# A hybrid decoder trunk on one core: meta queries left out, LayerNorm steps moved between engines, sample attention in float32r

## The reference, cut to what matters

```python
hp = concatenate([meta, x_prompt])         # 16 meta rows + 1024 prompt rows
hs = x_sample                              # 8 sequences x 8 new rows
# layer 0: pooling mixer, LN, SwiGLU, LN    layer 1: MLA, LN, SwiGLU, LN
def latent_attention(q_lat, q_pe, rows, q_pos, k_pos):
    c_kv, k_pe = rows[:, :256], rows[:, 256:]
    s = (q_lat @ c_kv.T + q_pe @ k_pe.T) * SCALE   # masked by position
    p = softmax(s)
    return p @ c_kv
# prompt: 1040 keys, 8 heads;  sample: 1024 cached rows (8 pages of 128) + 8 new ones per sequence
def mla_out(o_lat, w_uv, w_o): return (o_lat @ w_uv).reshape(n, t, 1024) @ w_o
def swiglu(h, w_gate, w_up, w_down): return (silu(h @ w_gate) * (h @ w_up)) @ w_down   # 1024 -> 2816 -> 1024
hp = LN(ALPHA * hp + mix); hp = LN(ALPHA * hp + swiglu(hp))      # the same for hs
return hp[:, 16:], hs, new states and latent cache rows
```

## Time and profile before

| what | us |
|---|---|
| median of the runs | 2528.48 |
| lowest run | 2527.64 |
| the profiled execution | 2538.14 |
| its span, first to last instruction | 2536.2 |
| TensorE busy | 2444.3 |
| VectorE busy | 1094.5 |
| GpSimd busy | 675.6 |
| ScalarE busy | 546.2 |

### The profile page before, as it was taken

The page is one execution under the profiler, slowest core; times in us unless marked ns, Lnnn a source line. Parts: engine busy times, 40 slices in busy tenths (PEclk is TensorE's granted clock), DMA queues, the critical chain, the costliest instruction groups (busy, mean ns, idle before and its releaser), DMA issues.

```text
span 2536.2 us, 36520 instructions
## 1 busy us (share of the span) xinstructions
PE 2444.3 (96%) x13475; PEld 2143.2 (85%) x13475; DVE 1094.5 (43%) x2030; ACT 546.2 (22%) x988; POOL 675.6 (27%) x448
## 2 busy tenths in 40 slices
PE   8999999999999979899999999989999999999996
PEld 8899999999999958587888884459999999999995
DVE  4443344334434562444555464423434433443446
ACT  3411111111111253232232223523111111111112
POOL 3532222322222330111112100333222322323225
PEclk9999999999999989999999999979999999999998
DMA  5111110111111010100000004511111011101111
GB/s 193 51 39 48 50 50 25 50 50 44 30 50 50 25 45 16 35 18 18 18 17 18 9 9 122 170 34 37 39 50 50 25 50 50 50 25 50 50 33 71
DMA packets 132430, 117.88 MB, mean 46 GB/s; under 512 B 8880, under 2 KB 119432, under 8 KB 132336
## 3 DMA queue, kind: packets, MB, share of 16 engines
q1 hardware_dynamic: 132352, 116.83, 14.8%
HBM read 110.94 MB, written 6.42 MB: 46 GB/s over the span
## 4 chain that ended last, share of the span: by engine, by line
PE 89%; DVE 4%; ACT 2%; issue 1%; ACTq 0%; DVEq 0%; POOL 0%
PE ps L682 23%; PE ps L683 23%; PE ps L684 22%; PE ps L1027 3%; PE ps L931 2%; PE ps L1014 1%; PE ps L1111 1%; PE ps L903 1%; PE ps L945 1%; PE ps L1086 1%; PE ps L936 1%; PE ps L977 1%; PE ps L1070 1%; DVE BNS L1484 1%; PE ps L980 1%
## 5 line engine op out<-in xcount | busy, mean ns | idle before, releaser
L682 PE MATMUL ps<-XH,WGH 128*128 128x368 f32 x2112 | 697.8, 330 | 4.0 <-DVE XL L1514 2.4
L683 PE MATMUL ps<-XL,WGH 128*128 128x368 f32 x2112 | 698.2, 331 | 0.0
L684 PE MATMUL ps<-XH,WGL 128*128 128x368 f32 x2112 | 695.8, 329 | 0.0
L1596 DVE TENSOR_TENSOR XR<-XR,ps 128x512 f32<-128x512 f32 x756 | 510.8, 686 | 8.3 <-PE ps L684 4.5
L1579 DVE TENSOR_TENSOR HF<-SG,ps 128x368 f32<-128x368 f32 x132 | 71.0, 538 | 917.7 <-PE ps L684 906.1
L682 PEld LDWEIGHTS ps<-XH,WGH 128*128 128x128 f32 x2112 | 397.2, 188 | 8.1 <-DVE XL L1514 2.8
L683 PEld LDWEIGHTS ps<-XL,WGH 128*128 128x128 f32 x2112 | 396.7, 188 | 1.9
L684 PEld LDWEIGHTS ps<-XH,WGL 128*128 128x128 f32 x2112 | 396.9, 188 | 0.0
L684 PE MATMUL ps<-WDH,HL 128*128 128x512 f32 (+1 forms) x792 | 313.5, 396 | 0.0
L682 PE MATMUL ps<-WDH,HH 128*128 128x512 f32 (+1 forms) x792 | 310.7, 392 | 2.0 <-DVE XR L1596 2.0
L683 PE MATMUL ps<-WDL,HH 128*128 128x512 f32 (+1 forms) x792 | 312.0, 394 | 0.0
(11 more groups left out here) (216 smaller groups left out, 2965.3 us busy)
## 6 DMA issues: line engine op xcount, KB each, us to landing
RAWG<-ffn_w_gate SPq DMA_DIRECT2D x44, 512.0 KB, 5.9
RAWG<-ffn_w_up SPq DMA_DIRECT2D x44, 512.0 KB, 6.9
RAWD<-ffn_w_down SPq DMA_DIRECT2D x44, 512.0 KB, 3.4
CR<-cache_mla_l SPq DMA_DIRECT2D x64, 160.0 KB, 2.6
XR<-x_prompt SPq DMA_DIRECT2D x8, 512.0 KB, 12.3
WOR<-mla_w_o SPq DMA_DIRECT2D x8, 512.0 KB, 3.2
WOA<-mla_w_o SPq DMA_DIRECT2D x1, 4096.0 KB, 17.2
o_y_prompt<-XR SPq DMA_DIRECT2D x8, 512.0 KB, 2.6
```

Source lines behind the costliest of these rows:

```text
L682: pe.matmul(out, w[0], x[0], start=start, stop=False)
L683: pe.matmul(out, w[0], x[1], start=False, stop=False)
L684: return pe.matmul(out, w[1], x[0], start=False, stop=stop)
L1596: dve.tensor_tensor(XR[0:r, t, ds], XR[0:r, t, ds], ps[0:r, 4 + 2 * w + half, :], ALU.add).then_inc(s_row[2 * l + 1], 1)
```

## The change

It does the following.

- **Meta queries.** The eight units of block 8 are gone; every head has eight units in one `ORDER`, with a new `NEXT_PLAN` and positions for GpSimd's work. The meta columns of `OT8` are zero.
- **Second FFN.** `turned`, `columns` and `third` put the sample rows at columns 1024 to 1087; the last third has 352 columns. The down products of tile 8 still have 80 rows.
- **LayerNorm.** After the first FFN GpSimd scales and shifts all nine tiles. Tile 8 of the LayerNorm behind the attention goes to VectorE. At the end VectorE takes tiles 6, 7, 8 whole, from the raw rows, in two fused operations a tile, behind its other work. The rows of tile 1 are normalized ahead of an FFN step that stood before them.
- **Sample attention.** Queries stand twice in 128 rows. Probabilities are split into a high part (ScalarE) and a low part (VectorE), side by side in 128 columns; the latents of the pages into a high copy `CH` (ScalarE) and a low part in place (GpSimd). The value product is 18 float32r matmuls of 256 columns; two matmuls with `IIF` (the identity twice) add the halves and transpose. The loop over steps is written out.
- **Order.** Pages of the first two sequences are loaded during attention. Page transposes of the first sequence stand between the first ten last output products, the other six stand in the sample tail. The first third of FFN unit 0 comes ahead of the sample output product. `w_o` is loaded head by head during the steps.

```diff
-LN_VECTOR = ((3, 6), (2, 5, 8), (), (2, 5, 8))
+LN_VECTOR = ((3, 6), (), (8,), (6, 7, 8))
 FIRST_TRANSPOSES = (({(1, 7): 6}, {(0, 5): 7, (1, 3): 8}, {}),
-                    ({(0, 1): 3, (0, 2): 4, (0, 5): 5, (1, 0): 6, (1, 3): 7}, {(0, 2): 8}, {}))
+                    ({(0, 6): 3}, {(1, 7): 8}, {}))
-        ORDER = ((7, 8, 6, 0, 5, 1, 4, 2, 3), (0, 7, 8, 6, 3, 5, 1, 4, 2))
+        ORDER = (7, 0, 6, 3, 5, 1, 4, 2)
...
+        FIRST_LAST, TAIL_SIDE = LAST_SIDE[:10], LAST_SIDE[10:]
+        def columns(l, t):
+            return slice(SEQ - META, SEQ + NS) if l == 1 and t == NT - 1 else cols(t)
+        def third(l, j):
+            return slice(j * TW, min(j * TW + TW, TOK - l * META))
+        def turned(k, t):
+            if k == 2 and t == NT - 1:
+                return slice(META, TAIL), slice(SEQ, SEQ + NS)
+            return slice(0, rows(t)), cols(t)
...
 # SP
+            load_pages(0, slot(0))
+            sp.wait_ge(h_s, NQ * (H - 1))
+            load_pages(1, slot(1))
+            sp.wait_ge(h_pv, NU)
+            load_pages(2, slot(2))
...
 # TensorE, sample_outputs
-                for k in range(NPAGE):
-                    pe.matmul(ps[0:NS, 6, 0:KVL], PST[:, k, :], CR[:, b, k, 0:KVL], start=(k == 0), stop=False)
+                for k in range(NPAGE + 1):
+                    if k in (0, NPAGE // 2, NPAGE):
+                        pe.wait_ge(c_nl, 3 * s + 2 * k // NPAGE + 1)
+                    high = CH[:, s % 2, k, :] if k < NPAGE else NRH[:, s % 2, :]
+                    low = CRL[b][:, k, 0:KVL] if k < NPAGE else NRL[:, b, :]
+                    pe.matmul(ps[:, 6, 0:KVL], PST[:, k, :], high, start=(k == 0), stop=False)
+                    ins = pe.matmul(ps[:, 6, 0:KVL], PST[:, k, :], low, start=False, stop=(k == NPAGE))
...
 # TensorE, second FFN
                 for j in range(3):
                     pe.wait_ge(s_xl, 2 * NT * l + 3 * j + 3)
                     gate_up_unit(l, 0, True, j, FIRST_TRANSPOSES[l][j])
+                    if l == 1 and j == 0:
+                        sample_product()
...
+            def sample_product():
+                pe.wait_ge(c_ov, 1)
+                pe.wait_ge(c_wo, 16 * H)
+                for half in (0, 1):
+                    ... # 16 passes each, as before, into banks 1 and 3
+                    if half == 0:
+                        ln_transposes(2, 4)
+                        ln_transposes(2, 5)
+                ins.then_inc(c_wm, 1)
+                ln_transposes(2, 6)
+                ln_transposes(2, 7)
+                pe.wait_ge(s_row[2], 1)
...
+            for s, between, behind in ((NSEQ - 2, TAIL_SIDE[0:2], TAIL_SIDE[2:3]),
+                                       (NSEQ - 1, TAIL_SIDE[3:5], TAIL_SIDE[5:6])):
                 probability_transposes(s)
+                for f in between:
+                    side(f)
+                sample_outputs(s, slot(s))
+                for f in behind:
+                    side(f)
                 sample_out_transposes(s)
...
 # ScalarE, sample_step
+                latents_high(s, 0, slot(s))
+                sample_probabilities(s, slot(s))
                 evacuate_pages(act, copy, s + 1, 4).then_inc(c_xa, 1)
+                if s > 0:
+                    sample_rows(s - 1, slot(s - 1))
+                latents_high(s, 1, slot(s))
+                if s in (0, 3):
+                    norm_rows([0] if s == 0 else [1, 2, 3])
...
 # VectorE
+            def ln_whole(k, t):
+                dve.scalar_tensor_tensor(XR[0:r, t, :], XR[0:r, t, :], MV[0:r, t, 0:1], GB[0:r, 0, :], ALU.subtract,
+                                         ALU.mult).then_inc(s_lv, 1)
+                ...
+                dve.scalar_tensor_tensor(XR[0:r, t, :], XR[0:r, t, :], RS[0:r, t:t + 1], GB[0:r, 1, :], ALU.mult,
+                                         ALU.add).then_inc(s_lv, 1)
+                if k == 3 and t == NT:
+                    for u in ln_vector(k):
+                        ln_whole(k, u)
...
+            ln_low(2, 3)
+            hidden_unit(1, 0, True, 0)
+            ln_low(2, 4)
+            ln_low(2, 5)
             dve.wait_ge(c_wm, 1)
+            ... # add the sample product to tile 8, its statistics
+            ln_low(2, 6)
+            ln_low(2, 7)
+            ln_scales(2, NT - 1, TAIL, NT - 1)
+            ln_gain(2, NT - 1)
+            ln_low(2, NT - 1)
 # GpSimd
+            for s in range(NSEQ):
+                latents_low(s, slot(s))
+                if s == NSEQ - 1:
+                    gate_up_low(1, 0, 0)
+                    gate_up_low(1, 0, 1)
+                ln_pool(2, POOL_TILES[s])
```

More of the change, by code:

```diff
@@ L212, in slot @@
         def slot(s):
-            return (s + 1) % 3
+            return s % 3
         def bank2(b, r, n=1024):
@@ L763, in gate_up_unit @@
                 pe.wait_ge(f_hf[l], 3 * n + j + 1)
-                cs = slice(j * TW, (j + 1) * TW)
+                cs = third(l, j)
+                n_cols = cs.stop - cs.start
                 for m, done in ((0, f_gmm[l]), (1, f_umm[l])):
@@ L1455, in _ @@
                 sample_queries(s, slot(s))
-            sample_step(0, 0)
-            with act.Fori(0, 2) as j:
-                for k in (1, 2, 3):
-                    sample_step(j, k)
+            for s in range(NSEQ - 1):
+                sample_step(s)
             for s in (NSEQ - 2, NSEQ - 1):
@@ L1599, in swiglu @@
             def swiglu(l):
-                hidden(l, 0, True)
+                for j in range(l, 3):
+                    hidden_unit(l, 0, True, j)
                 dve.wait_ge(s_xr, NT * (2 * l + 1))
@@ L1788, in sample_step @@
-                if not first:
+                if s < 5:
+                    ln_statistics(2, s, P, s)
+                if s > 0:
                     sample_columns(s - 1)
-                if k % 3 == 0:
-                    for n in (range(1) if first else range(1, 4)):
-                        ln_scales(2, s - k + n, P, slot(n))
-            dve.wait_ge(h_fd, len(SIDE_DVE))
-            for k in (1, 3, 5):
-                evacuate_pages(dve, copy, 0, k).then_inc(c_xd, 1)
-            sample_step(0, 0)
@@ L1821, in _ @@
-            for t in range(3, NT):
-                ln_low(2, t)
+                if s in (0, 3):
+                    for t in ([0] if s == 0 else (1, 2, 3)):
+                        ln_scales(2, t, P, t)
+            dve.wait_ge(c_kn, 1)
+            dve.tensor_tensor(IIF[:], IDF[:, 0:NS], IDF[:, NS:2 * NS], ALU.add).then_inc(c_ii, 1)
+            for n, f in enumerate(FIRST_LAST):
+                side_dve(f)
+                if n in PAGE_AFTER and PAGE_AFTER.index(n) % 2 == 1:
+                    evacuate_pages(dve, copy, 0, PAGE_AFTER.index(n)).then_inc(c_xd, 1)
@@ new lines, in _ @@
+            for s in range(NSEQ - 1):
+                sample_step(s)
+            sample_maxima(NSEQ - 1, slot(NSEQ - 1))
+            probabilities_low(NSEQ - 2)
+            sample_sums(NSEQ - 1, slot(NSEQ - 1))
+            for f in TAIL_SIDE[0:3]:
+                side_dve(f)
+            sample_columns(NSEQ - 2)
+            probabilities_low(NSEQ - 1)
+            for f in TAIL_SIDE[3:6]:
+                side_dve(f)
+            ln_statistics(2, 5, P, 5)
+            sample_columns(NSEQ - 1)
```

469 lines of the change are left out of this document (258 added, 211 removed).

## The result

The changed kernel takes 2489.81 us (median of 4 runs, 2489.32 to 2490.36), the kernel before 2529.18 beside it (four executions, one of them of 8561.45, the others 2527.64 to 2529.88). The ratio is put at 0.9826 with an interval of 0.9805 to 0.9847; the two medians alone give 0.9844, inside it. The kernel is faster, by a little less than 2%. Forecast were 2477.0, with a range of 2460 to 2495.

The account below looks back on a forecast made before the run. TensorE, busy 2444.3 of 2536.2 us, was taken as the bound. Seven terms summed to 51.5 us, giving 2486.6 for the profiled execution and 2477.0 for the median, with a range of 2460 to 2495.

Parts of the forecast that it names:

- case A: Whole kernel: the terms as summed give 2477 us, own range 2469 to 2486; chance 0.5.
- Rival C: After the first FFN: GpSimd becomes the bound, term 3 is -7 us, time 2490; chance 0.12.
- rival B: Tail: it keeps its gaps and low clock, term 6 is 0, time 2492; chance 0.2.
- term 2: Attention: eight of 72 units, the meta units, go; 7.4 us gained, bounds 3 and 9.
- term 5: Sample steps: cheaper float32r value products, a step from 15.40 to about 13.6 us; net 6.5 us gained.
- term 6: Tail, last sample scores to end of first gate/up block: 87.0 us becomes 72, 15 gained, bounds 0 and 20.
- Term 3: After the first FFN: GpSimd takes VectorE's scale and shift of three tiles; 6 us gained, bounds 0 and 11.
- Term 1: Second FFN: gate and up products lose 16 of 368 columns in the last third; 7.6 us gained.
- term 4: Start of the sample part: six page transposes move to the tail and gaps are filled; 5.5 us gained.
- term 7: End: VectorE sheds tiles 2 and 5, then runs six fused operations in 11.5 us; 3.5 us gained.
- Rival D: Sample steps: TensorE's clock falls to 1.2 GHz, steps double, +109 us, time 2601; chance 0.03.

Follow-up runs that it names:

- third tail run: Changed kernel with sequence 7's columns before tile 5's statistics, tile 0's transposes before the value-up product, half the sample output product before second-FFN unit 0: 2479.93 us.
- three tail runs: Changed kernel with VectorE's sequence 7 columns earlier, 2487.96 us; besides, tile 0's transposes earlier, 2485.03; besides, half the sample output product earlier, 2479.93.
- plan run: Changed kernel with the same side products of heads 1 to 6 spread otherwise over a head's eight units: 2475.83 us, ratio 0.9786.
- last version: Changed kernel with both the side products of heads 1 to 6 spread otherwise and the tail's new order in three places: 2465.68 us, ratio 0.9741.

## Why the prediction was right, and where it was not

The time lay in the range, 12.8 us above the forecast; it lay outside the 2469 to 2486 of case A, the sum, and by its number next to C's 2490 and B's 2492, of which C did not come and B came in part. That the kernel would stay within 2% of the one before had been given 0.47. Four of seven terms were near; of the three that missed, two nearly cancel (11.3 us too much in term 2, 8.2 too little in term 5), and that is luck.

**The base of the sum failed first.** The step "I make the sum against 2538.14 and take the same difference off the median" treats the 9.7 us as an offset that stays. They were low clock in the tail of that one execution, and term 6 counted them as gained: of the 12.8 us above the forecast they are 9.7. Against the execution for which it was made the sum, 2486.6, is 2.9 us off, and the tail gives 11.7; in an execution near the median it has 2.0 to give and not 15.

**Term 6, the tail (15, measured 2.0).** The work was priced well: 59.6 us forecast, 67.67 us busy in 75.1 with low clock, 61.2 without it (the third tail run). Besides the base, "I add 3 for low clock" is what failed: the stretch of 17.9 us was granted 0.52, which by these two busy times cost some 6.5 us; gaps were 7.4 us of the 9.4 forecast. Of rival B the low clock came and the gaps did not, and the three tail runs show what the clock hangs on in the changed kernel: with the waits filled by transposes and half a sample product, 9.9 us come back. The bound of 20 is a slip: 87.0 less 59.6 and half of 9.4 is 22.7. The gap feared ahead of the last third of unit 0 is 0.86 us.

**Term 2, the meta units (7.4, measured -3.9).** Work of 6.3 us did go. Outside even the lower bound of 3, "if half of that cover is missed", lies what happened: the prediction looked for exponentials that need cover, and the cover that was missing was for VectorE emptying two banks. The plan run shows it. The upper bound, that a new order of side products closes gaps, was the right idea: this order opened gaps, and that of the plan run closed them; with the work saved its attention is 10.7 us shorter than the kernel's before.

**Term 5, the sample steps (6.5, measured 14.7).** "A step goes from 15.40 to about 13.6" is where it was mis-sized: 12.64. The value products' saving was priced right (2.2 less 0.3 and 0.1, measured 1.55 for the pages alone). Missed was that one shape of operand throughout is cheaper: 0.58 a step is shown by the run with 64 columns; the other 0.6 lies by the timelines in the page transposes (0.59 to 0.35 for four, of which float32 brought back 0.09), and that was not run by itself. The "about 4.3 us" for which TensorE was to wait for ScalarE came to some 2 us more than before.

**Term 3 (6, measured 9.5).** Scale and shift alone are 5.8 at the latent product and 7.2 in the time. Most of the rest is the meeting of VectorE and GpSimd, which tile 1's new place, an unpriced move, avoids: against the execution of the kernel before in which VectorE started first (916.58) the shift is 6.5, near the forecast. Rival C, GpSimd as the bound, did not come: no wait for GpSimd's rows after the FFN. The rule against the move that the prediction weighed (the Trainium skill, page "GPSIMD Engine Reference", section "Engine selection") has the price right: 2.40 against 1.21 and 1.22 where VectorE is not held up (the run that gave scale and shift back), and 1.49 in the mean of the earlier trace rows. What decided was that GpSimd had the time and VectorE had not.

**Terms 1, 4 and 7** were 7.3 for 7.6 (21 of the 22 units lie in that stage), 6.0 for 5.5 and 3.6 for 3.5. Term 1 stands on the 7 ns in the timeline, term 4 on the stage alone; neither was run by itself. For term 7 the split was as forecast: two operations at the high price, four at the low. Its sum does not follow from its prices: two or three at 3.25 and the others at 1.49 are 12.5 to 14.2 us and not the 11.5 written. Measured are 11.7, because the low price turned out 1.27 to 1.34, so the hit is in part luck. Rival D did not come: 1.00 was granted in all steps, with waits of up to 1.0 us in them.

## What to carry to other kernels

Profile the kernel before twice: where two executions of one program differ, the stage that differs is not a stable term, and its low clock may not be there to gain. When short units of work are left out, look at what they stood between: two products into one bank need as much other work between them as the other engine takes to get to it and empty it. A wait that can't be shortened is worth filling with work that is due anyway, since what runs behind it may run at half the clock.

## What the runs showed of the hardware

- In the run with 64 columns of queries a change of the stationary operand's shape (128*128 to 128*64 or back) costs TensorE 0.1 to 0.2 us, while the width itself costs nothing: float32 passes of 512 columns are 0.44 us apart at either. The Trainium skill, page "TensorEngine Tiling (Array Packing)", section "Key Properties", says that changing the tiling mode drains the engine; whether a narrower operand is such a change, and whether the engine drains, no run here shows.
- In the run with float32 value products, one of 256 columns takes 0.43 us (two passes of 0.215); a float32r product of 256 columns takes 0.12, and the high and the low part together take two of these.
- Where operations of VectorE and GpSimd on 128x1024 float32 met, the one that started later took longer: VectorE's 3.46 us for 1.22 alone, GpSimd's 3.25 to 3.48 for 2.40. A lead of 0.01 us decided which, and with it the next 3 us.
- With nearly the same waits the tail of the kernel before was granted 0.80 in two profiled executions and 0.91 in a third, 9.7 us apart. In the changed kernel, with two waits of its tail filled (third tail run and the last version), the tail was granted 1.00, and the runs lay within 3.3 us.
